# Reordering a two-block kernel: one normalised input for all projections, filter generation beside a matrix product, and intermediate results kept in memory

## The chip, the cores and the metric

The kernel runs on one core of a Trainium2 chip. The metric is device microseconds (us) of one execution. A core has a matrix engine (PE, with its weight loads PEld), a vector engine (DVE), a scalar engine (ACT), a second elementwise engine (POOL) and a sync engine (SP) from whose queue this kernel issues all its DMA transfers. SBUF is the on-chip memory of 128 partitions, PSUM the accumulators that PE writes, in eight banks of 128x512 float32.

## The reference

Two transformer-like blocks run one after the other on a sequence of 1024 tokens with 1024 channels, all in float32. The change lies almost wholly in the first sub-layer of the first block:

```
u    = rms_norm(x, norm_mix_g)
proj = u @ w_in                                   # 1536 Hyena + 1024 q,k + 512 v + 512 o + 16 gates
hy   = short_conv_centred(proj[:, :1536])         # 3 taps along time, per channel
spec = rfft(two_sided(filter_mlp(t) * exp(-t*|delta|)))  # 2 orders, 2 directions, 512 channels
z, g1, g2 = split(hy)
for o, gate in enumerate((g1, g2)):
    z = gate * (irfft(rfft(z, 2L) * spec[o])[:L] + z * skip[o])
y_hy = group_rms_norm(z, hy_norm_g)
qk   = silu(short_conv_centred(proj[:, 1536:2560]))
y_ml = sigmoid(o_pre) * (mlstm(q, k, v, i, f) + reversed mlstm(...))
h    = x + concat(y_hy, group_rms_norm(y_ml)) @ w_out
```

`filter_mlp` is two layers of sin(freq * (w z + b)) with 64 hidden units over 33 features of t, and a third product to 2048 channels. After this come cross attention and a feed-forward layer, and the second block: adaptive norms, dilated and sparse attention, and a gated feed-forward layer. In the second block the norm ahead of the feed-forward is `h2 = rmsnorm(x, g) * (1 + sc2) + sh2`.

## The kernel before

Every large product is made of three passes: a float32 operand is split into a rounded high part (made by ACT) and the rest (made by DVE or POOL), and PE adds high*high, high*low and low*high (`mm3`, L187, L188, L189). A product of 1024x1024 by a tile of 128 columns is 48 such instructions, 8 slices by 3 passes by 2 halves of 512.

The program is a row of stages. Each is a block in which every engine has its own instruction list; engines meet through semaphores (named signals) inside it, and a barrier of all engines stands between two blocks. Nothing of the next stage starts before all five engines have left the one before, but loads that SP has issued ahead go on. The order of the work is written out by hand.

The first sub-layer, by stage (`first_block`, L2695):

1. `phase_first_norm`: x is loaded, normalised and transposed into `xt`.
2. `phase_conv_proj` (L557): twelve tiles of 128 Hyena columns, transposed. Per tile ACT writes the middle tap (L621), DVE adds the two others from PSUM (L645, L647), and PE transposes the result back (L597).
3. `phase_filter_hidden` (L665): the hidden layers of the filter (PE L699, L706; DVE L717 to L726; ACT's sine). Beside it PE reverses the second half of the tokens with a permutation matrix (L694).
4. For each order o: `phase_filter_time` (L759) makes the filter taps (PE L789, each a float32 product of 64 rows), ACT the decay (L805), DVE their product (L838, L839), POOL sum and difference of the two directions (L861, L862), DVE the fold of the two halves (L825, with a copy of row 0 at L829), and both its rounded parts (L797, L817). Then `phase_filter_spectrum`, `phase_signal_spectrum` and `phase_inverse_gate` do the transforms as products with tables that are streamed in 256 KB units (`Tables`: ACT L901, POOL L906).
5. `phase_group_norm` on y_hy; beside it x is loaded a second time (4 MB).
6. `phase_row_norm`: x is normalised and transposed a second time, since `xt` has been overwritten.
7. `phase_qk_proj` (8 tiles), `phase_vo` (32 rows by halves), `phase_gates` (one tile for 16 gate columns), `phase_gate_scans` (logarithms on ACT, four scans on DVE L1623 and L1628, 16 transposes L1638).
8. `phase_mlstm`, whose first product is L1679, then `phase_mix` and the output projection.

In the second block `phase_rows_gemm_norm(..., modulated=...)` makes the output projection and, row block by row block, the next norm (`StreamNorm`: DVE scales at L360, PE turns). There the shift sh2 is added by PE: two products with a picking matrix into each bank (L371, L372), and the turning is four accumulating products (L378) in place of four transposes (L376).

## Time and profile before

| what | value |
|---|---|
| median of 3 runs | 4065.82 us (4064.43 to 4067.47) |
| the profiled execution, whole time | 4063.24 us |
| its span, first to last instruction | 4061.4 us |
| busy share PE, PEld, DVE, ACT, POOL | 89%, 70%, 49%, 28%, 13% |
| mean granted clock of PE | 0.937 of full speed |

The profile is one execution. Busy shares are means over very different stages. A slice of the page in which PE reads 6 or 7 tenths marks stages in which it waits; PEclk, the clock that was granted, falls in the same slices (0.5 is 1.2 GHz, 1.0 is 2.4 GHz). Idle time is put in brackets behind the instruction that ended it, with the instruction or transfer that released it. In the rows "rounded" is a high or low part, "plain" a float32 tile.

### The profile page before, as it was taken

How to read it: one execution, taken by the hardware profiler on the slowest of the kernel's cores; microseconds unless marked ns; L12 is line 12 of the kernel's file. 1: busy time of each engine (PE TensorE's matmuls, PEld its weight loads, DVE VectorE, ACT ScalarE, POOL GpSimd, SP SyncE). 2: the span in 40 equal slices, each digit the busy share in tenths (PEclk: the TensorE clock that was granted, in tenths of full speed). 3: DMA queues.
4: the chain of work that ended last, by engine and by line, in shares of the span. 5: the costliest groups of instructions: out<-in, count | busy, mean ns of one | idle time of the engine just before them, and what ended most of it. 6: DMA issues, size and time to landing. Idle time of an engine off the chain costs nothing. (4 is left out here: it accounts for less than half of the span.)

```text
span 4061.4 us, 43012 instructions
## 1 busy us (share of the span) xinstructions
PE 3631.5 (89%) x16474; PEld 2856.8 (70%) x16474; DVE 1998.9 (49%) x3148; ACT 1121.2 (28%) x2006; POOL 541.7 (13%) x377
## 2 busy tenths in 40 slices
PE   7868696896978879999999998889989899999998
PEld 6736475773667757788888775766668777888886
DVE  3264645314744143555553438789975433333243
ACT  3233232323333132211211324124445321111112
POOL 0046564000010000101100100000034201000000
PEclk8969798897989999999999999999999999999999
DMA  2012123100022111323221211100000211111111
GB/s 94 27 33 74 42 79 106 31 32 4 1 91 83 57 47 34 97 93 121 93 93 60 84 52 37 47 20 22 11 14 1 99 37 52 52 49 49 47 52 52
DMA packets 210515, 220.07 MB, mean 54 GB/s; under 512 B 15523, under 2 KB 148548, under 8 KB 210098
## 3 DMA queue, kind: packets, MB, share of 16 engines
q1 hardware_dynamic: 210356, 217.90, 16.9%
q8 instruction: 106, 1.74, 0.2%
q14 instruction: 53, 0.43, 0.0%
HBM read 205.79 MB, written 11.55 MB: 54 GB/s over the span
## 5 line engine op out<-in xcount | busy, mean ns | idle before, releaser
L187 PE MATMUL psum<-rounded,rounded 128*128 128x512 f32 (+2 forms) x3936 | 1544.7, 392 | 216.5 <-POOL rounded L906 86.0
L188 PE MATMUL psum<-rounded,rounded 128*128 128x512 f32 (+2 forms) x3936 | 1536.2, 390 | 0.0
L189 PE MATMUL psum<-rounded,rounded 128*128 128x512 f32 (+2 forms) x3936 | 1534.1, 390 | 0.0
L187 PEld LDWEIGHTS psum<-rounded,rounded 128*128 128x128 f32 x3936 | 752.0, 191 | 384.0 <-POOL rounded L906 90.8
L189 PEld LDWEIGHTS psum<-rounded,rounded 128*128 128x128 f32 x3936 | 751.4, 191 | 153.1
L188 PEld LDWEIGHTS psum<-rounded,rounded 128*128 128x128 f32 x3936 | 751.9, 191 | 150.2 <-issue 0.2
L2634 DVE TENSOR_TENSOR plain<-psum,plain 128x512 f32<-128x512 f32 x432 | 288.5, 688 | 112.0 <-PE psum L189 110.6
L2645 DVE TENSOR_TENSOR plain<-psum,plain 128x512 f32<-128x512 f32 x44 | 30.4, 692 | 437.3 <-ACT plain L2554 437.3
L3052 POOL TENSOR_TENSOR plain<-plain,plain 128x128 f32<-128x128 f32 (+3 forms) x64 | 89.4, 1408 | 717.4 <-ACT plain L3123 695.4
L2626 DVE TENSOR_TENSOR rounded<-plain,rounded 128x512 fp32r<-128x512 f32 x108 | 97.2, 900 | 174.8 <-ACT rounded L2543 174.7
L2915 DVE MAX8 plain<-plain 128x8 f32<-128x384 f32 (+5 forms) x192 | 170.6, 889 | 4.0
L2917 DVE MATCH_REPLACE8 plain<-plain,plain 128x384 f32<-128x384 f32 (+5 forms) x192 | 168.1, 876 | 0.0
L2554 ACT ACTIVATE plain<-psum 128x512 f32<-128x512 f32 x44 | 26.3, 599 | 470.3 <-PE psum L189 470.3
L2612 POOL TENSOR_TENSOR plain<-plain,plain 128x1024 f32<-128x1024 f32 x22 | 53.4, 2429 | 748.2 <-DMA plain<-in_w_down_dram 748.2
L2990 PE MATMUL psum<-plain,plain 64*128 64x512 f32 (+7 forms) x384 | 151.2, 502 | 0.0
L906 POOL TENSOR_TENSOR rounded<-plain,rounded 128x512 fp32r<-128x512 f32 x96 | 133.3, 1402 | 128.9 <-ACT rounded L901 128.7
L2600 POOL TENSOR_TENSOR plain<-plain 128x512 f32<-128x512 f32 x64 | 67.2, 1050 | 606.2 <-ACT plain L2556 606.2
L2556 ACT ACTIVATE plain<-psum 128x512 f32<-128x512 f32 x64 | 38.3, 598 | 380.3 <-PE psum L189 380.3
L2576 ACT ACTIVATE rounded<-plain 128x1024 fp32r<-128x1024 f32 x54 | 57.1, 1057 | 278.6 <-DMA plain<-in_ff_w_dram 160.6
L3071 DVE CUSTOM_DVE_ANT_0 plain<-psum,plain 128x128 f32<-128x128 f32 (+7 forms) x128 | 96.4, 753 | 69.1 <-PE psum L2990 38.1
L3125 ACT ACTIVATE plain<-plain,plain 128x128 f32<-128x128 f32 (+7 forms) x128 | 98.8, 772 | 56.7 <-DVE plain L3074 56.0
L901 ACT ACTIVATE rounded<-plain 128x512 fp32r<-128x512 f32 x96 | 58.7, 629 | 178.3 <-DMA plain<-in_c_fwd_dram 103.5
(284 smaller groups left out, 3935.8 us busy)
## 6 DMA issues: line engine op xcount, KB each, us to landing
plain<-in_ff_w_dram SPq DMA_DIRECT2D x64, 512.0 KB, 5.5
plain<-in_w_ada_dram SPq DMA_DIRECT2D x96, 256.0 KB, 3.1
plain<-in_w_gu_dram SPq DMA_DIRECT2D x44, 512.0 KB, 4.9
plain<-in_w_in_dram SPq DMA_DIRECT2D x36, 512.0 KB, 3.7
plain<-in_c_fwd_dram SPq DMA_DIRECT2D x64, 256.0 KB, 2.6
plain<-in_w_down_dram SPq DMA_DIRECT2D x22, 512.0 KB, 3.2
plain<-in_c_inv_dram SPq DMA_DIRECT2D x32, 256.0 KB, 2.6
plain<-in_x_dram SPq DMA_DIRECT2D x2, 4096.0 KB, 15.5
```

The costliest lines, as they stand in the source:

```text
L187: nc.tensor.matmul(out, wh, xh, start=first, stop=False)
L188: nc.tensor.matmul(out, wh, xl, start=False, stop=False)
L189: return nc.tensor.matmul(out, wl, xh, start=False, stop=last)
L906: self.core.nc.gpsimd.tensor_tensor(w.lo, w.raw, w.hi_raw, ALU.subtract).then_inc(S["ft_lo"].sem, 1)
L2626: nc.vector.tensor_tensor(ft[b].lo[:, f, cols], full[half], ft[b].hi_raw[:, f, cols], ALU.subtract).then_inc(S["ft_lo"].sem, 1)
L2634: nc.vector.tensor_tensor(hv, ps[:, 4 + t % 4, :], hv, ALU.add).then_inc(S["dve_free"].sem, 1)
L2915: nc.vector.max(best, sc).then_inc(self.done, 1)
L2917: nc.vector.match_replace(out=sc, in_to_replace=best, in_values=sc, imm_value=TAKEN).then_inc(self.done, 1)
L2990: last = nc.tensor.matmul(ps[:, 2 * (n % 2) + a // BANK, 0:b - a], q, k[:, a:b], start=True, stop=True)
L3052: nc.gpsimd.tensor_tensor(tb[n % 2][:, 0:w], biases[h % 2][:, L - w:L], sel_tile(core, i), ALU.add).then_inc(S["pool_done"].sem, 1)
L3071: nc.vector.tensor_tensor_reduce(out=sc[n % 2][:, 0:w], in0=pair(n, w), in1=b, scale=SCALE, scalar=-3.0e38, op0=ALU.add, op1=ALU.max, accu ...
L3125: nc.scalar.activation(sc[n % 2][:, 0:w], sc[n % 2][:, 0:w], ACT.Exp, bias=stat[:, n % 16, 1:2], accum_out=stat[:, n % 16, 2:3]).then_inc( ...
```

## The change

All products with `xt` now stand together right after the first norm: q and k with the gates as a ninth tile, then v and o with the scans beside them, then the convolution's projection with the filter generation beside it. What the mLSTM needs later (q, k, v, o, the running maximum, two column tables: `Kept`) is written to memory and loaded again during the second inverse transform and the group norm. The folded filters (2 x 4 MB) are also written to memory and loaded again, the first ahead of its spectrum, the second during the first inverse transform. The second load of x, its second norm, `phase_filter_hidden`, both `phase_filter_time`, `phase_gates` and `phase_gate_scans` are gone as stages. The reversal of the second half is made by reading PSUM backwards in the convolution, so the permutation products are gone. In the second block the shift is added by POOL (`StreamNorm.add`) in place of PE.

```diff
 def first_block(core):
+    phase_first_norm(core, x, xt, first_columns(core, weight_tiles(core, QK_RING_KB), w_rows, HY_COLS))
+    kept = Kept(core)
+    phase_qk_proj(core, xt, w_in, kept, first_pieces(core, VO_KB, w_rows[:, :, base:base + DH], count=1))
+    phase_vo(core, xt, w_in, kept, first_columns(core, weight_tiles(core, CONV_RING_KB), w_rows, 0))
-    phase_conv_proj(core, xt, w_in, hy)
-    phase_filter_hidden(core, hy)
+    filters = phase_conv_proj(core, xt, w_in, hy, kept)
     for o in range(2):
-        phase_filter_time(core, tables, o)
-        phase_filter_spectrum(core, tables, hy)
+        phase_filter_spectrum(core, tables, hy, filters.folds[0] if o == 0 else None)
         phase_signal_spectrum(core, tables)
-        phase_inverse_gate(core, tables, hy, o)
+        phase_inverse_gate(core, tables, hy, o, (lambda sp: load_folds(core, sp, filters.folds[1])) if o == 0 else (lambda sp: load_kept(core, sp, kept, True)))
-    phase_row_norm(core, x, xt, "norm_mix_g", 70, 74, [core.sig["x_ready"]], ...)
-    phase_qk_proj(core, xt, w_in, first_pieces(...))
-    phase_vo(core, xt, w_in)
-    phase_gates(core, xt, w_in)
-    phase_gate_scans(core)
     phase_mlstm(core)
```

The convolution's block, PE's list and DVE's list (F0 is 3, NF is 8):

```diff
@@ phase_conv_proj, tensor
                     for half in range(2):
                         last = mm3_cols(nc, ps[:, 2 * (n % 2) + half, :], ring[n % 4], ...)
+                        if half == 0 and 1 <= f <= NF:
+                            filters.taps(pe, f - 1, 1)
...
                     for t in range(TT):
-                        last = nc.tensor.transpose(ps[:, 4 + 2 * (m % 2) + t // 4, ...], tmp[m % 2][:, cuts[t]:cuts[t] + P], core.ident)
+                        last = nc.tensor.transpose(ps[:, 4 + t // 4, ...], tmp[m % 2][:, t * P:(t + 1) * P], core.ident)
+                if n < 2:
+                    filters.hidden(pe, n)
+                if 0 <= f < NF:
+                    filters.taps(pe, f, 0)
@@ phase_conv_proj, vector
+                if 1 <= f <= NF:
+                    filters.weigh(dve, f - 1, 1)
                 dve.wait_ge(S["act_done"].sem, S["act_done"].at(n + 1))
+                for out, src in ((t[:, 1:513], pr[:, 0:512]), (t[:, 513:L], pr[:, L - 2:511:-1])):
+                    last = nc.vector.scalar_tensor_tensor(out=out, in0=src, scalar=w0, in1=out, ...)
...
+                if 1 <= f <= NF:
+                    filters.fold(dve, f - 1)
+                if 0 <= f < NF:
+                    filters.weigh(dve, f, 0)
@@ class Filters
+    def taps(self, pe, f, m):
+        pe.wait_ge(S["windowed"].sem, S["windowed"].at(n))     # n = 2 * f + m
+        for half in range(2):
+            last = nc.tensor.matmul(ps[:, 6 + half, :], self.hid[...], self.w3[...], start=True, stop=True)
+        last.then_inc(S["tap_done"].sem, 1)
+    def store(self, sp, f):
+        sp.wait_ge(S["pair_folded"].sem, S["pair_folded"].at(f + 1))
+        sp.dma_start(self.folds[o]..., self.out).then_inc(S["fold_stored"].sem, 16)
```

The spectrum stage now makes the rounded parts of the folds itself, and the second block's norm adds its shift on POOL:

```diff
@@ phase_filter_spectrum
+            for n in range(4):                       # scalar
+                act.wait_ge(S["fold%d" % n].sem, S["fold%d" % n].at(16))
+                nc.scalar.activation(blocks(fold.hi, n), blocks(raw, n), ACT.Copy).then_inc(S["fold_hi"].sem, 1)
+            for n in range(4):                       # vector
+                nc.vector.tensor_tensor(blocks(fold.lo, n), blocks(raw, n), blocks(fold.hi_raw, n), ALU.subtract)...
@@ class StreamNorm
+    def add(self, pool, t, row):
+        pool.wait_ge(S["row_scaled"].sem, S["row_scaled"].at(t + 1))
+        nc.gpsimd.tensor_tensor(tmp, tmp, row, ALU.add).then_inc(S["row_added"].sem, 1)
```

How the lists move. DVE, one steady tile of the convolution before: the low part of a weight tile (L634), the two outer taps, and one copied column.

```order
L645 SCALAR_TENSOR_TENSOR plain_38400_1025_328<-psum,plain_896_128_50,plain_38400_1025_328 128x1023 [waits act_done]
L647 SCALAR_TENSOR_TENSOR plain_38400_1025_328<-psum,plain_896_128_50,plain_38400_1025_328 128x1023 [waits dve_chain]
L649 COPY plain_38400_1025_328<-plain_38400_1025_328 128x1 [waits dve_chain]
L634 TENSOR_TENSOR rounded_48640_1024_72<-plain_48640_1024_73,rounded_47616_1024_71 128x1024 [waits w_hi]
L645 SCALAR_TENSOR_TENSOR plain_39488_1025_329<-psum,plain_896_128_50,plain_39488_1025_329 128x1023 [waits act_done]
```

The same engine and place in the changed kernel, from one `act_done` to the next (L872 and L875 are the outer taps in halves, L713 the fold, L684 and L685 the taps times the decay, L852 the low part):

```order
L872 SCALAR_TENSOR_TENSOR plain_38400_1024_1473<-psum,plain_896_128_50,plain_38400_1024_1473 128x512 [waits act_done]
L872 SCALAR_TENSOR_TENSOR plain_38400_1024_1473<-psum,plain_896_128_50,plain_38400_1024_1473 128x511
L875 SCALAR_TENSOR_TENSOR plain_38400_1024_1473<-psum,plain_896_128_50,plain_38400_1024_1473 128x513 [waits dve_chain]
L875 SCALAR_TENSOR_TENSOR plain_38400_1024_1473<-psum,plain_896_128_50,plain_38400_1024_1473 128x510
L713 TENSOR_TENSOR plain_35328_2048_1488<-plain_30208_2048_1485 128x512 [waits fold_stored,pair_summed]
L713 TENSOR_TENSOR plain_35328_2048_1488<-plain_30208_2048_1485 128x512 x3
L684 TENSOR_TENSOR plain_32256_2048_1486<-psum,plain_34304_1024_1487 128x512 [waits pair_summed,tap_done,decay_ready]
L685 TENSOR_TENSOR plain_32256_2048_1486<-psum,plain_34304_1024_1487 128x512
L852 TENSOR_TENSOR rounded_43776_1024_64<-plain_43776_1024_65,rounded_42752_1024_63 128x1024 [waits w_hi]
L684 TENSOR_TENSOR plain_32256_2048_1486<-psum,plain_34304_1024_1487 128x512 [waits pair_summed,tap_done,decay_ready]
L685 TENSOR_TENSOR plain_32256_2048_1486<-psum,plain_34304_1024_1487 128x512
```

Four instructions per tile have become thirteen, and the first L684 pair is what the signal `windowed` tells PE.

PE in the second block's norm before, the end of one row block's turning and the products behind it (L371 and L372 add the shift, L378 turns):

```order
L378 MATMUL psum<-plain_0_896_49,plain_5632_2048_9062 128x128 x4
L371 MATMUL psum<-rounded_51072_8_21830,rounded_50816_128_21828 128x512
L372 MATMUL psum<-rounded_51072_8_21830,rounded_50944_128_21829 128x512
L378 MATMUL psum<-plain_0_896_49,plain_5632_2048_9062 128x128 x4
L187 MATMUL psum<-rounded_42496_2048_9617,rounded_17920_8192_21649 128x512
```

PE at the same place in the changed kernel (L387 is a transpose, L190 the first of the three passes):

```order
L192 MATMUL psum<-rounded_42496_2048_9295,rounded_26112_8192_21328 128x512
L387 MATMUL psum<-plain_0_896_49,plain_5632_2048_8740 128x128 [waits row_added,row_lo]
L387 MATMUL psum<-plain_0_896_49,plain_5632_2048_8740 128x128 x7
L190 MATMUL psum<-rounded_42496_2048_9295,rounded_17920_8192_21327 128x512
```

The four shift products per row block are gone from PE, and its turning waits for POOL's `row_added` where it waited for DVE's `row_scaled`.

## Rows read from the trace of the kernel before

**Rows 1.** Busy time by stretch: window, length, PE, PEld, DVE, ACT, POOL, PEclk, DMA, GB/s.
```profile
42.00:184.00 142.00, 141.80 (x662) 118.22 (x663) 42.54 (x45) 32.13 (x32) 0.00 (x0) 0.99 0.11 30
...
445.40:506.30 60.90, 27.67 (x32) 10.49 (x32) 47.04 (x59) 17.27 (x28) 27.95 (x19) 0.52 0.08 26
506.30:672.00 165.70, 148.30 (x630) 121.43 (x630) 70.19 (x85) 51.71 (x89) 103.15 (x71) 0.94 0.24 72
672.00:729.50 57.50, 21.78 (x114) 19.20 (x113) 41.59 (x57) 22.85 (x37) 8.03 (x8) 0.63 0.36 120
729.50:819.40 89.90, 89.90 (x384) 73.86 (x384) 26.25 (x21) 22.43 (x21) 0.00 (x0) 0.97 0.12 36
...
828.90:918.60 89.70, 89.67 (x384) 73.77 (x384) 6.88 (x3) 15.77 (x19) 0.00 (x0) 0.97 0.07 24
918.60:969.60 51.00, 15.51 (x66) 12.39 (x65) 17.25 (x11) 9.36 (x9) 0.99 (x2) 0.67 0.07 7
```

**Rows 2.** Timeline of PE: start, length, instruction, count [idle before <-releaser].
```profile
224.53 15.72 PE L789 MATMUL psum<-plain,plain 64*128 64x512 f32 x18 [8.76 <-DMA plain<-in_hy_filt_w_dram]
...
277.57 0.80 PE L187 MATMUL psum<-rounded,rounded 128*128 128x512 f32 x1 [25.37 <-POOL rounded L906]
...
394.83 0.80 PE L187 MATMUL psum<-rounded,rounded 128*128 128x512 f32 x1 [13.00 <-POOL rounded L906]
...
686.80 7.38 PE L1241 MATMUL psum<-plain,plain 128*128 128x128 f32 x48 [14.78 <-DVE plain L1214]
...
963.34 1.96 PE L1638 MATMUL psum<-plain,plain 64*128 64x64 f32 x16 [21.84 <-DVE plain L1629]
...
969.60 3.78 PE L1679 MATMUL psum<-plain,plain 64*128 64x512 f32 x4 [4.29 <-DMA plain<-in_c_sel_dram]
```

**Rows 3.** Timeline of PE, the convolution's transposes of tiles 0, 1 and 10.
```profile
65.64 1.03 PE L597 MATMUL psum<-plain,plain 128*128 128x128 f32 x8
...
77.43 1.03 PE L597 MATMUL psum<-plain,plain 128*128 128x128 f32 x8
...
183.40 1.03 PE L597 MATMUL psum<-plain,plain 128*128 128x128 f32 x8
```

**Rows 4.** Timelines of PE and DVE in the two filter stages.
```profile
212.07 3.70 PE L694 MATMUL psum<-plain,plain 128*128 128x512 f32 x8
...
242.21 0.41 DVE L829 COPY plain<-plain 1x512 f32<-1x512 f32 x1
...
248.61 4.62 DVE L825 TENSOR_TENSOR plain<-plain 128x512 f32<-128x512 f32 x4 [1.19 <-POOL plain L862]
...
270.37 2.48 DVE L825 TENSOR_TENSOR plain<-plain 128x512 f32<-128x512 f32 x4
```

**Rows 5.** DMA issues: tile, queue, count, KB each, us to landing.
```profile
plain<-in_x_dram SPq DMA_DIRECT2D x1, 4096.0 KB, 13.8
...
saved_x<-plain SPq DMA_DIRECT2D x8, 512.0 KB, 2.6
```

**Rows 6.** Timelines of POOL and DVE, where one stage hands over to the next.
```profile
676.31 4.04 POOL L1201 TENSOR_TENSOR plain<-plain 128x512 f32<-128x512 f32 x4 [7.76 <-POOLq L1094]
...
690.88 4.94 DVE L1225 TENSOR_TENSOR plain<-psum,plain 128x512 f32<-128x512 f32 x9
...
826.59 2.29 DVE L1557 TENSOR_TENSOR rounded<-plain,rounded 128x2048 fp32r<-128x2048 f32 x1 [3.30 <-ACT rounded L1530]
```

**Rows 7.** Timelines of DVE (second block) and PE (first block), and the page's POOL group.
```profile
3274.36 1.28 DVE L360 SCALAR_TENSOR_TENSOR plain<-plain,plain,plain 128x1024 f32<-128x1024 f32 x1
...
3280.55 1.28 DVE L360 SCALAR_TENSOR_TENSOR plain<-plain,plain,plain 128x1024 f32<-128x1024 f32 x1
...
1237.12 1.03 PE L376 MATMUL psum<-plain,plain 128*128 128x128 f32 x8
...
1240.75 1.03 PE L376 MATMUL psum<-plain,plain 128*128 128x128 f32 x8
...
L2612 POOL TENSOR_TENSOR plain<-plain,plain 128x1024 f32<-128x1024 f32 x22 | 53.4, 2429 | 748.2 <-DMA plain<-in_w_down_dram 748.2
```

731 lines of the change are left out of this document (390 added, 341 removed).

## The prediction, on record before the changed kernel ran

> **What bounds the kernel now.** I read the page first: PE is busy 89% of the span, no other engine over half, and its idle time stands in the slices of the first quarter. The busy times by stretch come next [rows 1]. In the long products (42 to 184, 729.5 to 819.4, 828.9 to 918.6) PE is busy all the time at a clock of 0.97 to 0.99, so nothing can be won there but fewer instructions. Between them lie stretches in which PE works half the time or less at 0.5 to 0.67. The timeline of PE then says what ended each wait [rows 2]: a DMA, the last table unit of POOL, the DVE of a norm, the scans. So the first 970 us are a row of full products with gaps between, and the price of a stage is either its PE time or, where PE waits, its whole length, since a barrier closes it. The chain of waits on the page agrees: it is nearly all PE.
>
> **The sum, as a new timetable.** I lay the changed stages end to end up to the mLSTM's first product, which starts at 969.6 now [rows 2]. Behind it only one place changes.
>
> 1. The first norm stays: 42.0.
> 2. q and k: eight tiles took 89.9 [rows 1], so nine take 89.9 * 9/8 = 101.1. The gates' own stage goes. Its small loads are first in SP's queue and are wanted six tiles later. The spills of q and k sit in the same queue ahead of the loads for v and o, but each tile's 512 KB store lands in about 2.6 [rows 5] and a tile lasts 11.2. At 143.1.
> 3. Gap to v and o. It was 9.5: last tile's taps and silu, then ACT's and DVE's parts of the first weights, the latter 2.29 [rows 6]. Now only two bias additions stand behind the last product, so 7.4. At 150.5.
> 4. v and o: 89.7 [rows 1], to 240.2. The scans filled the wait of 21.84 in [rows 2]; with the logarithms they are some 19 us on ACT and DVE. DVE does them ahead of the third piece of weights, which PE wants some 45 us after the start, half the stage. Hidden; if that cover failed the price would be up to 21.84.
> 5. Gap to the convolution: its first tiles are loaded ahead, so one ACT and one DVE part of 1024 columns and the barrier, 4. At 244.2.
> 6. The convolution's own 142.0 [rows 1]; tile to tile is 77.43 - 65.64 = 11.79 [rows 3]. PE gets 32 tap products and 4 hidden ones. Four such float32 products took 3.70 at the full clock [rows 4], 0.9 each, against 15.72 / 9 = 1.75 each at half clock in the old filter stage [rows 2]. That is 36 * 0.9 = 32.4 and 1 for the 16 transposes: 33.
>    Waits of PE inside it: the taps of one half need the banks that DVE frees with its product `windowed`. After a tile's last product, ACT writes the middle tap (1.3), DVE adds the outer ones (2.6), folds the pair before (2.48 for four [rows 4]) and only then multiplies (1.3): 7.7. PE comes back to those banks after 0.8 of transposes, 1.8 of taps and half a tile, 5.5: 8.1. So it just fits. The two pairs with copied rows need 4 * 0.41 more [rows 4] and some waits, about 2 each past the fit. I take 5 in all. Lower bound 0. Upper bound: the reversed PSUM reads are in no row. If they ran at half speed, DVE and ACT would need 1.8 more per tile, and if POOL shared DVE's time in the fold it would be 4.62 for 2.48 [rows 4]: 2 more; with the first 5 that is 8 * 3.8 + 5 = 35. I take 5, since the scans before also read backwards and nothing on POOL runs at the time of the fold. So 142 + 33 + 5 = 180, to 424.2.
> 7. Gap to the first spectrum. Taps and fold behind the last tile 6.5; the last 1 MB store, by 512 KB in 2.6 [rows 5], 5; barrier; then table units and the first quarter of the fold, 2 MB, by the 4 MB that landed in 13.8 [rows 5] about 7.5; ACT's and DVE's parts of 2048 columns 1.9 and 2.29 [rows 6]. That is 24. Bounds 18 (store and loads in half the time) and 36 (store at the 4 MB transfer's whole latency). At 448.2.
> 8. The three transform stages of order 0 keep their 445.4 - 277.6 = 167.8 [rows 1, 2], to 616.0. The load of the second fold, 4 MB, now stands ahead of the table units in SP's queue. The inverse starts PE at 394.83 [rows 2], with four units there; the stage began some 2.3 before, the first unit's rounding on ACT and POOL. 4 MB are down 13.8 later [rows 5], about 406, then the fifth unit, ACT and POOL 4 more: 410, and PE takes its fifth unit at about 411. So 0, at most 8 per inverse if the written memory reads slower.
> 9. Gap to the second spectrum. It was 60.9 [rows 1]. Of it 4.3 remain for the gate and the barrier, as 676.31 against 672.0 in the second order [rows 6], then three table units on ACT 1.7, the fold's high and low part 4.2 and 1 for POOL beside it: 11.3. The clock falls to 0.5 before every such start now too [rows 1, 2], so its price is in the old stages already. At 627.3.
> 10. Order 1: 165.7 [rows 1], to 793.0. The load of q, k ahead of its inverse is like that in 8.
> 11. Group norm until DVE's last row, 690.88 + 4.94 [rows 6], and the start: 696.3 - 672.0 = 24.3. 4.7 MB are loaded beside it where x's 4 MB took 13.8; issued near 676.5 they are there by 693. At 817.3.
>
> 969.6 - 817.3 = 152.3 us. Where it comes from: the second norm with its hand-over 35, gates and scans about 40, the first pair of filter stages about 30 (94 to 24 and 38 more of PE), the second about 50.
>
> 12. Second block. A row block of the modulated norm takes 3280.55 - 3274.36 = 6.19, one in the plain norm 1240.75 - 1237.12 = 3.63 [rows 7]; PE has no idle time in either, so the four shift products and the slower turning cost 2.56 per row. POOL's addition is 128x1024, 2.43 [rows 7], and lies between DVE's scaling and PE's turning. In the six rows beside products PE has two rows of slack for it. The last two rows are turned with nothing beside them: there PE saves as much again, about 5, and the addition costs that back, once at the first turning and once at the last. Best case 6 * 2.56 = 15, worst 0 if POOL and DVE slow each other as in [rows 4], where four folds took 4.62 beside POOL and 2.48 alone. I take 11.
>    The Trainium skill, SBUF — State Buffer, "Who interferes with whom", says that a DVE instruction with two SBUF inputs and a GpSimd instruction that reads SBUF exclude each other for the whole instruction. The 4.62 against 2.48 agrees in direction. By that rule a scaling that meets an addition waits it out, 1.28 + 2.43 = 3.7 a row, still under 6.19; by it the sum would hardly change unless DVE's other work does not fit either, which is the rival below.
>
> Together 163.3. Against the profiled execution, 4063.24 - 163.3 = 3899.9; it ran 2.6 under the median of the runs, so 3902.5, and I say 3902.
>
> **Rivals.**
> A. The convolution is paced by DVE. For it: thirteen instructions a tile where four stood, and the fit of 8.1 against 7.7 in step 6. Against it: DVE was busy 42.54 of 142 there [rows 1] and gets about 53 more, 8 * (2.5 + 2.6) for folds and windows and 12 for the hidden layers, on 180. Price 35 for my 5: 3902 + 30 = 3932.
> B. The reloads are late. For it: 12 MB more through one queue, twice ahead of the table stream. Against it: the 13.8 for 4 MB. Step 7 at 36, 8 for each inverse, 4 in the group norm: 12 + 16 + 4 = 32, so 3934.
> C. POOL's addition gives nothing in the second block: DVE waits for POOL in each row and the row stays near 6. The POOL and DVE rows above speak for it, the row's 3.7 against it. 3902 + 9 = 3911.
> D. Better than forecast: step 6 without waits, step 7 at 18, step 12 at 15: 3902 - 5 - 6 - 4 = 3887.
> E. Slower than before. One mechanism: the ring taps, window, addition, fold, store, in which each link waits for the next before its buffers are free. If it ran serially, PE would stand for each of the 16 half pairs. It would have to lose 163 / 16 = 10.2 us at each to undo the gain. The old filter stage, which is this ring on its own, needed 277.57 - 224.53 = 53 for eight half pairs with its low parts, 6.6 each [rows 2], so even wholly exposed it costs about 106, and the time would be near 4000. Only store and reload at several times the measured durations would carry it over 4066.
> F. The change does not do what it says: a stage that I count as gone still costs. The order of SP, PE and DVE leaves no room for it.
>
> **How the numbers follow.** Main forecast 3902 with its own range of 3888 to 3916: 0.60. A 0.09, B 0.11, both together in part 0.03 (up to 3950). C 0.06. D 0.09. E 0.01 for over 4066, and 0.01 for an exposed ring that still gains. The range 3880 to 3934 leaves out a little over one in ten. A measurement of this kernel can tell 0.2%, 8 us. Every case but E's first half is far below 4058: faster 0.985, same 0.005, slower 0.01.
>
> **What would show it.** PE's first convolution product after v and o near 244, the first spectrum near 448, the second near 627, the mLSTM's first product near 817. In the convolution, tiles with taps 15.3 to 15.8 apart; a wait of PE on `windowed` (the DVE product L685) of over 1 us in most tiles is A. A wait for a fold or table transfer in either inverse is B. In the second block turnings 3.7 to 4.3 apart; near 6 is C. The forecast is wrong if the gaps of steps 7 and 9 sum to over 50, or if the clock in the long products falls below the 0.97 of now.

## The result

The changed kernel takes 3914.41 us (median of four runs, 3911.34 to 3921.62), the kernel before 4065.7. The ratio on record is 0.9632, with a 95% interval of 0.962 to 0.9643 (the two medians alone give 0.9628). The forecast was 3902 us with a range of 3880 to 3934, so the time lies inside it, 12 us above the 3902. Measured once more, five runs beside the version at the end of the experiments, the kernel after took 3914.98 (3913.14 to 3922.1); one of these is what is called its second profile below.

The profiled execution took 3914.14 us with a span of 3912.3; before it was 4063.24 and 4061.4. So 149.1 us are to be accounted for, where the prediction said 163.3.

### The profile page after: what moved, and what is told of

Same layout as the page of the kernel before. It is cut to its first block and busy times, and to the rows that moved or that the text cites. A ratio compares the mean times of both kernels' runs of the same rounds, so it can differ in the third digit from the quotient of the medians.

```text
span 3912.3 us, 42554 instructions
## 1 busy us (share of the span) xinstructions
PE 3565.9 (91%) x16290; PEld 2817.0 (72%) x16290; DVE 1961.9 (50%) x3111; ACT 1093.4 (28%) x1949; POOL 550.7 (14%) x385
## 5 line engine op out<-in xcount | busy, mean ns | idle before, releaser
L190 PE MATMUL psum<-rounded,rounded 128*128 128x512 f32 (+2 forms) x3936 | 1546.1, 393 | 186.9 <-POOL rounded L933 37.7
L190 PEld LDWEIGHTS psum<-rounded,rounded 128*128 128x128 f32 x3936 | 751.2, 191 | 366.5 <-POOL rounded L933 40.2
## 6 DMA issues: line engine op xcount, KB each, us to landing
plain<-fold SPq DMA_DIRECT2D x8, 1024.0 KB, 10.1
```

Of the source, the lines that this page charges most:

```text
L190: nc.tensor.matmul(out, wh, xh, start=first, stop=False)
```

## The profile after

The busy time by stretch, as in [rows 1] (window, length, PE, PEld, DVE, ACT, POOL, granted clock, DMA share, GB/s). In the order of time: q, k and gates; v and o with the scans; the convolution with the filters; the gap to the first spectrum; the gap between the two orders; the group norm up to the mLSTM; and, last, the second block's output projection with its norm.

```profile
41.90:142.20 100.30, 100.28 (x432) 82.48 (x432) 30.07 (x24) 25.67 (x24) 0.00 (x0) 0.98 0.25 75
...
149.40:239.60 90.20, 90.18 (x384) 74.05 (x384) 19.56 (x10) 21.49 (x24) 0.00 (x0) 0.97 0.25 85
...
243.40:427.40 184.00, 181.28 (x746) 129.90 (x747) 95.92 (x138) 51.98 (x65) 45.66 (x34) 0.99 0.22 73
427.40:452.80 25.40, 2.71 (x17) 2.07 (x15) 7.51 (x9) 9.03 (x9) 3.71 (x3) 0.59 0.61 226
620.30:631.20 10.90, 0.03 (x1) 0.03 (x1) 6.96 (x7) 6.66 (x6) 3.72 (x3) 0.63 0.07 24
800.70:824.80 24.10, 8.29 (x50) 8.12 (x49) 19.60 (x31) 1.63 (x2) 8.02 (x8) 0.65 0.54 201
3048.70:3158.20 109.50, 99.50 (x448) 81.44 (x448) 44.89 (x45) 23.94 (x49) 27.98 (x10) 0.95 0.23 82
```

The gaps are what to look at. Before, TensorE stood or ran at half clock for 60.9 us between the orders; now it is 10.9. Of the stretch of 57.5 between the second order and q, k [rows 1] the 24.1 of the group norm are left, and the one of 51.0 with the gate products and scans is gone. VectorE, busy for 42.54 of 142.0 in the old convolution, is busy for 95.92 of 184.0 in the new one, and TensorE is still busy for 181.28.

The waits of TensorE from there to the mLSTM, which answer to [rows 2] (start, length, instruction, count, idle time before and what ended it):

```profile
321.99 1.98 PE L666 MATMUL psum<-plain,plain 64*128 64x512 f32 x4 [1.36 <-DVE plain L685]
387.64 1.98 PE L666 MATMUL psum<-plain,plain 64*128 64x512 f32 x4 [1.36 <-DVE plain L685]
452.78 0.79 PE L190 MATMUL psum<-rounded,rounded 128*128 128x512 f32 x1 [19.14 <-DVE rounded L1039]
...
569.04 0.79 PE L190 MATMUL psum<-rounded,rounded 128*128 128x512 f32 x1 [12.30 <-POOL rounded L933]
585.97 0.50 PE L190 MATMUL psum<-rounded,rounded 128*128 128x512 f32 x1 [1.69 <-POOL rounded L933]
631.17 0.79 PE L190 MATMUL psum<-rounded,rounded 128*128 128x512 f32 x1 [10.91 <-DVE rounded L1039]
...
766.37 0.50 PE L190 MATMUL psum<-rounded,rounded 128*128 128x512 f32 x1 [1.54 <-POOL rounded L933]
824.78 1.95 PE L1754 MATMUL psum<-plain,plain 64*128 64x512 f32 x4 [1.04 <-PEq L1248]
```

Only two of the sixteen tap pairs wait (L666, before 321.99 and 387.64), 1.36 us each; a float32 product stands in two records, so a pair counts x4. The mLSTM's first product stands at 824.78 and stood at 969.60 [rows 2]: 144.8 us earlier.

The transfers of the folded filters, from the page (instruction, count, KB each, us to landing):

```profile
fold<-plain SPq DMA_DIRECT2D x8, 1024.0 KB, 4.7
plain<-fold SPq DMA_DIRECT2D x8, 1024.0 KB, 10.1
```

And the second block's norm: VectorE's scaling (L363), POOL's addition (L369) and TensorE's turning (L387), which answer to [rows 7].

```profile
3122.86 1.28 DVE L363 SCALAR_TENSOR_TENSOR plain<-plain,plain,plain 128x1024 f32<-128x1024 f32 x1
3125.58 2.15 DVE L363 SCALAR_TENSOR_TENSOR plain<-plain,plain,plain 128x1024 f32<-128x1024 f32 x1
...
3135.19 1.28 DVE L363 SCALAR_TENSOR_TENSOR plain<-plain,plain,plain 128x1024 f32<-128x1024 f32 x1
...
3151.51 2.20 DVE L363 SCALAR_TENSOR_TENSOR plain<-plain,plain,plain 128x1024 f32<-128x1024 f32 x1
```
```profile
3124.30 2.35 POOL L369 TENSOR_TENSOR plain<-plain,plain 128x1024 f32<-128x1024 f32 x1 [41.71 <-DVE plain L363]
...
3150.28 2.34 POOL L369 TENSOR_TENSOR plain<-plain,plain 128x1024 f32<-128x1024 f32 x1 [2.60 <-DVE plain L363]
```
```profile
3126.80 1.06 PE L387 MATMUL psum<-plain,plain 128*128 128x128 f32 x8 [2.11 <-POOL plain L369]
3130.46 1.03 PE L387 MATMUL psum<-plain,plain 128*128 128x128 f32 x8
3135.47 1.06 PE L387 MATMUL psum<-plain,plain 128*128 128x128 f32 x8 [1.24 <-POOL plain L369]
...
3152.77 1.94 PE L387 MATMUL psum<-plain,plain 128*128 128x128 f32 x8 [3.88 <-POOL plain L369]
3156.28 1.94 PE L387 MATMUL psum<-plain,plain 128*128 128x128 f32 x8 [1.56 <-POOL plain L369]
```

The turnings stand 3.5 to 5.0 apart, where row blocks stood 6.19 apart [rows 7], and from the first product to the end of the last turning the stage takes 109.5 where it took 117.7 (3191.3 to 3309.0). TensorE waits for POOL at five of the eight, 2.11 + 1.24 + 1.20 + 3.88 + 1.56 = 10.0 us (the 1.20, at 3144.14, falls into the gap of the rows shown).

## The experiments

Two questions were put first. Which part of the change gives how much? And what paces the new convolution, TensorE or the ring of taps, window, addition and fold?

### The shift on POOL alone

The kernel before with one part of the change (cut at the dots):

```diff
@@ class StreamNorm
+    def add(self, pool, t, row):
+        pool.wait_ge(S["row_scaled"].sem, S["row_scaled"].at(t + 1))
+        nc.gpsimd.tensor_tensor(tmp, tmp, row, ALU.add).then_inc(S["row_added"].sem, 1)
...
+        if self.added:
+            pe.wait_ge(S["row_added"].sem, S["row_added"].at(t + 1))
+        else:
+            pe.wait_ge(S["row_scaled"].sem, S["row_scaled"].at(t + 1))
...
-    norm = StreamNorm(..., BEHIND, shift=shift and shift.operands())
+    norm = StreamNorm(..., BEHIND, added=modulated is not None)
...
-                    pe.wait_ge(S["shift_lo"].sem, S["shift_lo"].at(1))
```

> The kernel before, with one part of the change alone: in the second block's modulated norm POOL adds the shift to the scaled rows, and TensorE's four shift products per row are gone. Theory (the parts add up, and nothing that happens before the second block touches this one): the stretch from the second block's output projection to the end of its norm shortens by the same 8.2 us as between the two profiles, so 4065.8 - 8.2 = 4057.6 us, ratio 0.9980. The turnings of the last rows stand 3.7 to 5 us apart. Rival 1 (POOL and VectorE slow each other so much that only the full change, whose DMA queues look different, gains): within 2 us of the kernel before. Rival 2 (what the prediction took, 11 us of 15): 4054.8 us. All the rest of the 151 us gained, about 143, must then be the new order of the first block.

Measured: 4060.3 us (11 runs) against 4065.79, ratio 0.9987, interval 0.9978 to 0.9996. The busy time of the same stretch, of this kernel and of the kernel before:

```profile
3197.05:3306.50 109.45, 99.46 (x448) 81.36 (x448) 44.86 (x45) 23.94 (x49) 28.00 (x10) 0.95 0.23 81
```
```profile
3191.30:3309.00 117.70, 117.17 (x544) 93.03 (x544) 43.48 (x46) 24.17 (x51) 8.97 (x2) 0.98 0.20 72
```

The stage shortens by 8.25 us, as much as in the full change, with the same waits in the same places. TensorE's busy time falls by 17.7 for the 96 records that are gone, and 9.5 of that come back as waiting for POOL. The time as a whole fell by 5.5, and the interval reaches from 1.6 to 8.9, so it takes in the 8.2 (0.9980) and leaves out the 11 of rival 2; that rival 1, 2 us at most, falls is shown by the stage, hardly by the interval. In the profiled execution this kernel was already 5.7 us late at this first product, 3.4 of it from an earlier stage, the one that begins at 1401.56 (1399.20 in the kernel before), where its instructions are those of the kernel before: 115.6 at a granted clock of 0.91 against 112.3 at 0.94. The kernel after takes 115.1 there, and 112.5 in two of the runs below, so this is a difference of one execution to the next. The first theory stands. The rest of the 149.1, some 141, must come from the first block's new order.

### The filters behind the convolution instead of beside it

```diff
-    FIRST = 3
+    FIRST = 12
...
-                        if half == 0 and 1 <= f <= NF:
-                            filters.taps(pe, f - 1, 1)
...
+            for f in range(NF + 1):
+                if f >= 1:
+                    filters.weigh(dve, f - 1, 1)
+                    filters.fold(dve, f - 1)
+                if f < NF:
+                    filters.weigh(dve, f, 0)
```

> The kernel after, but with all taps, windows, additions and folds of the filters behind the convolution's last tile instead of beside tiles 3 to 11; the two hidden layers stay beside. Same instructions, buffers and stores. Theory (beside the tiles the ring costs only TensorE's own time for the products, about 31 us of tap pairs, and on its own it costs its full latency): one pair then needs window product 1.3, tap pair 1.93, window product 1.3, POOL's two additions about 2.6, fold 2.5 and the hand-overs about 0.4, together 10 us; 8 pairs 80 us. The tiles' part falls by 31 us of taps, 3 of waits and 2 of interruptions to about 148. So 3914 + 80 - 36 = 3958 us. Rival 1 (the price of an exposed ring as in the prediction, 6.6 us per half pair, 106 in all): 3914 + 106 - 36 = 3984 us. Rival 2 (it matters little where the ring stands, the gain was all in the dropped stages and their starts): within 8 us of 3914.

Measured: 3977.94 us, ratio 0.9784 (0.9769 to 0.9799), so 63.5 more than the kernel after, where the theory said 44 and rival 1, with the prediction's price of an exposed ring, 70. It is nearer to the rival. Rival 2 falls. The two parts, tiles alone and ring alone, by stretch:

```profile
242.50:388.50 146.00, 145.98 (x676) 118.74 (x677) 55.94 (x70) 40.15 (x48) 0.00 (x0) 0.99 0.14 40
396.00:490.20 94.20, 60.33 (x65) 18.52 (x64) 39.56 (x66) 13.74 (x18) 38.30 (x32) 0.50 0.22 81
```

And three tap pairs in the ring:

```profile
401.17 3.78 PE L666 MATMUL psum<-plain,plain 64*128 64x512 f32 x4 [1.45 <-DVE plain L685]
...
414.48 3.78 PE L666 MATMUL psum<-plain,plain 64*128 64x512 f32 x4 [4.31 <-DVE plain L685]
...
425.99 3.78 PE L666 MATMUL psum<-plain,plain 64*128 64x512 f32 x4 [2.52 <-DVE plain L685]
```

The ring alone takes 94.2, not 80. The missing term is the clock: the granted clock is 0.50 over the whole stretch, the 1.2 GHz level, and a tap pair takes 3.78 instead of 1.98. The theory's chain has one tap pair in each of its eight turns; with 3.78 for its 1.93 it gives 80 + 8 * 1.85 = 94.8. That is a sum that fits, no run had the ring alone at the full clock. Of the 16 pairs 14 wait for VectorE's window product, as expected, 1.44 at one half and 2.52 or 4.31 at the other; the first waits for nothing and one for the second half of the taps' weights, 3.62. TensorE is busy for 60.33 of the 94.2, at half speed.

The tiles end with the transposes of tile 10 at 389.45, 146.93 after their first product; in the kernel after it is 427.24 - 243.36 = 183.88. So beside the tiles the ring costs 36.95 us, and apart it costs 94.2 and a gap of 23.55 for 19.14. The same work in another place is worth a good 60 us (271.2 - 209.4 = 61.8 from the convolution's first product to the first spectrum's). It is the largest part of the gain that a run cut out. The rest of the first block, some 80 us (the second norm, the gates and scans as stages of their own, the starts between them), is read from the stretches that have gone or become shorter in the table; no run took it apart.

### Twice the tap products

```diff
-        for half in range(2):
+        for half in (0, 0, 1, 1):
             last = nc.tensor.matmul(ps[:, 6 + half, :], ...)
```

> The kernel after, with every one of the 32 tap products issued twice in a row into the same bank. Theory (TensorE is what paces the convolution with its filters): 16 more pairs at the measured 1.93 us each, 30.9, less up to 2.7 for the two waits of 1.36 us that VectorE's longer cycle removes: 28 to 31 us more, 3942 to 3945 us. The tile distance rises from about 16.05 to about 19.9. Rival (rival A of the prediction, VectorE's thirteen instructions pace it): half or more of the extra TensorE work disappears into waits, under 16 us more, below 3930 us.

Measured: 3936.48 us, ratio 0.9678 (0.9663 to 0.9693), 22 more than the kernel after. The first of TensorE's doubled pairs in one tile and in the next:

```profile
353.94 3.70 PE L666 MATMUL psum<-plain,plain 64*128 64x512 f32 x8
...
373.47 3.70 PE L666 MATMUL psum<-plain,plain 64*128 64x512 f32 x8
```

A doubled pair takes 3.70, and no wait of 1 us is left. From one tile to the next it is 373.47 - 353.94 = 19.53, against 16.05 in the kernel after (346.54 - 330.49 there): 3.48 for two more pairs. So a second pair right behind the first costs 1.74, not the 1.93 that I had taken from the whole interruption. By that the sum is 16 * 1.74 - 2.7 = 25.1; from the convolution's first product to the first spectrum's the trace has 234.54 against 209.42, 25.1. The 22 of the medians lies within their spread. TensorE paces the convolution; rival A of the prediction would have hidden most of this. The expectation's lower end, 28, was missed by the size of a pair.

That also splits the price of the taps. Without them a tile takes 11.79 [rows 3], with them 16.05: 2.13 for each pair. 1.74 are the products, by the price of the second pair, and 0.39 are left for the interruption of the long rounded products. What in the interruption costs them, no run shows.

### The window product later

```diff
                 if 0 <= f < NF:
+                    dve.wait_ge(S["tap_done"].sem, S["tap_done"].at(2 * f + 1))
+                    dve.wait_ge(S["decay_ready"].sem, S["decay_ready"].at(2 * f + 1))
+                    for at, width in ((146, 512), (148, 512), (197, 256)):
+                        nc.vector.tensor_tensor(core.view(at, width), ps[:, 6, 0:width], filters.decay[:, 0, 0:width], ALU.mult)
                     filters.weigh(dve, f, 0)
```

> The kernel after, with three more VectorE products (128x512, 128x512, 128x256, about 0.62 + 0.62 + 0.35 = 1.6 us) ahead of the first window product of each of the 8 pairs; their results are used by nobody. Theory (in six of the eight tiles the window product is ready only 0.4 us before TensorE wants its banks; in the other two TensorE already waits 1.36): TensorE waits 1.2 us more in six tiles and 1.6 in two, 6 * 1.2 + 2 * 1.6 = 10.4, so 3914 + 10 = 3924 us (3921 to 3928), and a wait of about 1.2 us on L685's successor shows in every tile. Rival (there is real slack, and the two waits are only the copied rows): the extra work hides, 2 * 1.6 = 3 us at most, 3914 to 3917 us.

Measured: 3926.57 us, ratio 0.9662 (0.9647 to 0.9677), 12 more. TensorE's waits, in a tile with copied rows and in one without:

```profile
323.48 1.98 PE L666 MATMUL psum<-plain,plain 64*128 64x512 f32 x4 [2.89 <-DVE plain L685]
...
342.28 1.98 PE L666 MATMUL psum<-plain,plain 64*128 64x512 f32 x4 [1.08 <-DVE plain L685]
```

The added products delay TensorE by 1.08 in a tile without copied rows, and by 2.89 - 1.36 = 1.53 in one with them, where no slack was left. So the fit is real, and its slack is 1.53 - 1.08 = 0.45 us a tile. The prediction had 8.1 against 7.7 for it.

The sum of the expectation comes near the measured 12 in part by luck. Only five tiles without copied rows wait, not six; the first pair of all does not. And the two tiles with copied rows grow by 3.1, from 17.5 to 20.6, though their wait grew by 1.5. The rest is the clock. Behind the wait of 2.89 TensorE's long products run near the lower level for 3.7 us:

```profile
325.40:329.10 3.70, 3.70 (x11) 2.91 (x11) 1.29 (x2) 0.00 (x0) 3.70 (x4) 0.57 0.00 0
```

The granted clock is 0.57 there; in the kernel after, behind its wait of 1.36, it is 1.00 (324.0 to 327.7).

### The window product ahead of the fold

This kernel and the next three have one execution each. The kernel after lies between 3911 and 3922 us in its own nine, so a total that is 2 to 6 us lower says little; the readings go by the traces.

```diff
-                if 1 <= f <= NF:
-                    filters.fold(dve, f - 1)
                 if 0 <= f < NF:
                     filters.weigh(dve, f, 0)
+                if 1 <= f <= NF:
+                    filters.fold(dve, f - 1)
```

> The kernel after, with VectorE's order in the convolution's tile turned round: the next pair's first window product stands ahead of the fold of the pair before, not behind it. Theory (the two waits of TensorE of 1.36 us on L685, at 322.0 and 387.6 of the kernel after, come from the fold with its four copied rows that stands ahead of the product): both waits go, the convolution takes 184.0 - 2.7 = 181.3 us from its first product to the last, no wait on L685 over 0.5 us is left. Rival (the product is late for another reason, the tail of VectorE's taps): the waits stay at 1 us or more, or others come up since POOL's additions now wait for the later fold.

Measured: one run at 3908.55 us. VectorE in one tile, now with the window product (L685 is its second half) ahead of the fold (L713):

```profile
332.19 0.68 DVE L685 TENSOR_TENSOR plain<-psum,plain 128x512 f32<-128x512 f32 x1
332.79 2.49 DVE L713 TENSOR_TENSOR plain<-plain 128x512 f32<-128x512 f32 x4
```

No tap pair waits any more. The tile-10 transposes stand 423.40 - 242.68 = 180.72 behind the first product instead of 183.88, 3.2 less where 2.7 was said, and the first spectrum 207.04 behind it instead of 209.42. The theory holds; the two waits were the fold's copied rows. In the kernel after such a fold lasts from 316.46 to 320.73, 4.27 for the 2.49 of a plain one; less the slack of 0.45 that makes 1.33, and the wait is 1.36.

### The gap to the first spectrum

The last store of the fold is waited for only ahead of the third quarter of the reload, and table units and quarters are loaded and rounded in turns:

```diff
-            sp.wait_ge(S["fold_stored"].sem, S["fold_stored"].at(16 * NF))
...
     for n, q in enumerate(FOLD_ORDER):
+        if all_stored is not None and n == 2:
+            sp.wait_ge(core.sig["fold_stored"].sem, all_stored)
+        if tables is not None:
+            sp.dma_start(tables.ring[n].raw, core.ap["c_fwd"][n]).then_inc(tables.loaded[n], 16)
         sp.dma_start(raw[:, 4 * q:4 * q + 4, :], ...)
...
-            for u in range(3):
-                tables.high(act, u)
             for n in range(4):
+                if n < 3:
+                    tables.high(act, n)
```

> The kernel after, with two edits in the gap to the first spectrum (25.4 us, which the prediction put at 24 by a sum of a store, a barrier and 2 MB of loads). First, the last 1 MB store of the fold is not waited for at the end of the convolution, only ahead of the reload's third and fourth quarter. Second, the first three table units and fold quarters are issued, and rounded on ScalarE, in turns instead of all units first. Theory (the gap is that chain of transfers): 4 us go with the store's wait and 2 to 3 with the order, the gap is 18 to 20 us. Rival (the gap is the barrier and the engines' roundings, the transfers are beside them): less than 2 us.

Measured: one run at 3912.39 us. From tile 10's transposes to the first spectrum it is 449.21 - 428.11 = 21.10, in the kernel after 452.78 - 427.24 = 25.54. That is 4.4 less, where the theory said 6 to 7 and the rival under 2: the chain of transfers is right as a cause and the size is off. (In the second profile of the kernel after the gap is 26.18.) The two edits were not run apart. ScalarE in this kernel, first table unit and first quarter:

```profile
441.69 0.63 ACT L928 ACTIVATE rounded<-plain 128x512 fp32r<-128x512 f32 x1 [6.78 <-DMA plain<-in_c_fwd_dram]
444.92 1.91 ACT L1021 ACTIVATE rounded<-plain 128x2048 fp32r<-128x2048 f32 x1 [2.61 <-DMA plain<-fold]
```

And what all transfers moved, in 40 slices of 0.875 us from 425 to 460:

```profile
GB/s 0 0 0 0 0 0 0 0 0 0 0 0 49 384 386 211 194 403 330 262 335 377 449 431 396 417 461 405 393 435 433 375 84 0 0 59 241 0 0 0
```

The loads no longer wait for the store, and from the 13th slice to the 33rd the transfers have no pause. The first quarter's rounding starts 16.8 us behind tile 10's transposes instead of 21.25 (448.49 in the kernel after). With the wait gone, the bytes ahead of the first quarter remain, at the rate that the slices show.

Three more things stand in this trace, and the first two reach the last kernel below. The second quarter of the fold is now late for TensorE, by 0.87 at 455.79. The rounding in turns also shortens the gap to the second spectrum, from 10.91 to 9.09. And the convolution took 1.4 more, one of its tiles 19.1 instead of 17.5, since behind the second wait of 1.36 (at 386.91) the clock fell:

```profile
388.90:392.60 3.70, 3.70 (x10) 2.88 (x11) 1.29 (x2) 0.00 (x0) 3.70 (x4) 0.54 0.22 76
```

The granted clock is 0.54 there and 1.00 in the same place of the kernel after. It fell in the run of the reloads in pieces too (0.54). So a wait inside the long products can cost as much again as it lasts, in some executions and not in others.

### The reloads in pieces

```diff
-            ahead(sp)
-            tables.load(sp, ap["c_inv"], ap["c_fwd"] if o == 0 else None)
+            tables.load(sp, ap["c_inv"], ap["c_fwd"] if o == 0 else None, ahead)
...
             sp.dma_start(self.ring[u % 4].raw, src).then_inc(self.loaded[u % 4], 16)
+            if u - 4 < len(between):
+                between[u - 4](sp)
```

> The kernel after, with the 4 MB reloads in the two inverse transforms issued in pieces, one behind each of the first table units, instead of whole ahead of the fifth unit. Theory (rival B of the prediction in small: TensorE's waits of 1.69 at 586.0 and 1.54 us at 766.4 are the table units queued behind the reload): both waits fall under 0.3 us, the two inverses together take 3 us less. Rival (they are the start of the table stream itself, since the rounding has to begin anew in every stage): both waits stay above 1 us.

Measured: one run at 3908.33 us. Both waits are gone. The stretch from the inverse's first product to the next stage, for either order, in this kernel and in the kernel after:

```profile
570.12:630.28 60.16, 49.25 (x210) 40.33 (x211) 23.49 (x24) 16.44 (x23) 35.17 (x26) 0.93 0.42 142
747.29:811.47 64.18, 49.40 (x211) 40.43 (x211) 29.47 (x33) 11.44 (x19) 39.62 (x31) 0.90 0.50 176
```
```profile
569.04:631.17 62.13, 49.54 (x210) 40.28 (x210) 25.80 (x24) 16.31 (x23) 36.03 (x26) 0.91 0.39 138
749.21:815.47 66.26, 49.95 (x210) 40.51 (x210) 29.61 (x33) 11.27 (x19) 40.21 (x31) 0.89 0.47 168
```

1.97 and 2.08 less, 4.05 together. Against the second profile of the kernel after, whose two waits are 0.63 and 1.45 and whose stretches are 61.50 and 66.04, it is 1.34 and 1.86. So the fifth table unit did stand behind the reload, and the price of whole reloads is 1.3 to 2.1 us an inverse.

### The addition in halves

```diff
-        nc.gpsimd.tensor_tensor(tmp, tmp, row, ALU.add).then_inc(S["row_added"].sem, 1)
+        for q in range(2):
+            part = tmp[:, q * BANK:(q + 1) * BANK]
+            nc.gpsimd.tensor_tensor(part, part, row[:, q * BANK:(q + 1) * BANK], ALU.add).then_inc(S["row_added"].sem, 1)
...
         for q in range(2):
+            if self.added:
+                pe.wait_ge(S["row_added"].sem, S["row_added"].at(2 * t + q + 1))
```

> The kernel after, with POOL's addition of 128x1024 in two of 128x512, each released to TensorE by itself. TensorE waits for POOL at five of the eight turnings of the second block's norm, 2.11 + 1.24 + 1.20 + 3.88 + 1.56 = 10.0 us. Theory (it waits for the end of the addition, so half of it, 1.2 us, goes at each): 5 to 6 us less, the stage from the output projection's first product to the end of the last turning takes 104 us instead of 109.5. Rival (VectorE and POOL exclude each other on their shared operands: VectorE's scalings then meet one of two POOL instructions more often, and some of the gain is eaten): 2 to 3 us less.

Measured: one run at 3909.95 us; the stage took 107.67 from its first product to the last turning's end (3048.01 to 3155.68), 1.8 less than 109.5. Theory and rival both asked for more. TensorE's first row in halves, POOL's addition and VectorE's second scaling:

```profile
3124.82 0.63 PE L389 MATMUL psum<-plain,plain 128*128 128x128 f32 x4 [1.03 <-POOL plain L371]
3125.96 0.66 PE L389 MATMUL psum<-plain,plain 128*128 128x128 f32 x4 [0.50 <-POOL plain L371]
```
```profile
3123.40 2.50 POOL L371 TENSOR_TENSOR plain<-plain,plain 128x512 f32<-128x512 f32 x2 [41.50 <-DVE plain L363]
```
```profile
3124.69 2.30 DVE L363 SCALAR_TENSOR_TENSOR plain<-plain,plain,plain 128x1024 f32<-128x1024 f32 x1
```

The first half starts 1.3 earlier against the stage's first product, but the row ends when the second half of the addition and then half a turning have ended: 0.72 behind the addition (3126.62 against 3125.90) instead of 1.21 (3127.86 against 3126.65). By the ends of the turnings the three waited rows among the products gain 0.3 to 0.6 each, and the last two rows 0.6 together. I had counted the earlier start as the gain.

### All four together

> The kernel after with the four edits of the runs above together: VectorE's window product ahead of the fold, the last store of the fold behind the first reloads, table units and fold quarters in turns, the reloads of the inverses in pieces behind the first table units, POOL's addition in halves. By their own traces they take 2.4 (first spectrum minus the convolution's first product, 209.42 to 207.04), 4.4 (the gap to the first spectrum, 25.54 to 21.10), 2.0 + 2.1 (the two inverses up to the next stage) and 1.8 us (the second block's output projection up to the next stage), 12.7 together. Theory (each waits on the path for itself, so they add up): 3914.4 - 12.7 = 3901.7 us, ratio to the kernel before 0.9596. Rival (the edits share what they gain, since the DMA queues are full at 380 to 450 GB/s in the gap): half of it, 3908 us.

> The kernel after once more, in the same rounds on the same chip as the version with the four edits, so that these two can be compared. Expected as in the first measurement, 3914.4 us, 3911 to 3917.

Measured: 3903.97 us (3899.83 to 3906.3), ratio to the kernel before 0.9602 (0.9589 to 0.9615); the kernel after in the same rounds 3914.98, ratio 0.9634 (0.9621 to 0.9647). This version beats both kernels, by 11.0 us the one after. The theory of a plain sum said 12.7, with a rival of about 6. One wait shows where part of the rest may be: the second quarter of the fold comes late behind the first.

```profile
444.27 0.79 PE L190 MATMUL psum<-rounded,rounded 128*128 128x512 f32 x1 [14.67 <-DVE rounded L1064]
450.86 0.50 PE L190 MATMUL psum<-rounded,rounded 128*128 128x512 f32 x1 [1.59 <-DVE rounded L1064]
```

From the convolution's first product to the mLSTM's it is 572.55 instead of 581.42, 8.9 less where the parts had 10.9. Up to the first spectrum nothing is lost, 202.18 instead of 209.42, 7.2 for the parts' 6.8. Behind it the sum had left out two things that both stand in the run of the gap alone: this wait (0.87 there, 1.59 here, 0.45 more in the second order) and the shorter gap to the second spectrum (9.08 for 10.91), which nearly cancel. The other 2 us are spread over the transform stages, which differ by about 1 us each between the two profiles of the kernel after; what they are is not shown.

## Why the prediction was right, and where its 14 us are

**The timetable to the mLSTM** (steps 1 to 11) said 817.3 and came out at 824.8. Steps 1 to 5 are within 0.8 each and end at 243.4 where 244.2 was said: norm 41.9, q, k and gates 100.3, gap 7.2, v and o 90.2, gap 3.8. The logarithms and scans are hidden entirely, as step 4 said: no wait of TensorE in that stage.

**Step 6, the convolution, is the largest miss up to there**, 184.0 for 180. Its waits were over-estimated (2.7 for 5) and its products under-estimated, so the two errors took something from each other. The term "36 * 0.9 = 32.4 and 1 for the 16 transposes" is the mis-sized one. Sixteen pairs cost 2.13 each, 34.1, where 32 * 0.9 = 28.8 stood, because 0.39 come with each interruption; doubling the taps showed that the products alone are 1.74. The hidden layers and transposes cost 146.93 - 141.4 = 5.5 where 4.6 stood, 141.4 being the same stretch before (42.0 to 183.40 [rows 1, 3]). The reversed reads of PSUM, which the prediction had in no row, are no slower than it took: the two outer taps last 1.41 each, 2.8 for the 2.6 of its sum. The mechanism was right: TensorE paces it, the window product fits by 0.45 us, the copied rows do not. The tiles stand 16.05 apart, not the 15.3 to 15.8 of the forecast, and rival A is refuted by the doubled taps, which did not disappear into waits, and by the two waits where it asked for one in most tiles.

**Step 7, the gap,** took 25.4 for 24, with the last store landing at about 439 and the first quarter's rounding at 448.49. Rival B was right in kind in steps 8 and 10, in a size of 1.3 to 2.1 us an inverse instead of 8. Step 8 still gave 167.5 for 167.8, step 9 gave 10.9 for 11.3.

**Step 10, the second order,** took 169.5 for 165.7. 1.54 are the wait at 766.37. Most of the rest is the clock: after the three starts of this order TensorE's products are at full speed 5.7, 4.9 and 3.9 us later, in the old second order, from which the 165.7 were taken, 3.5, 3.8 and 3.1 us later. Half of the 4 between them is lost, about 2. The prediction had the fall before every start in its old stages, but not that its end moves.

It moves from one execution to the next. In the first order of this profile the three are 3.2, 3.2 and 3.1. In the second profile of the same kernel it is the first order that is late, with 6.0, 5.1 and 3.9, and the second has 3.9, 4.0 and 3.5. From the second order's first product to the transposes of the group norm it took 184.3 in one profile and 182.5 in the other, with 180.5 in the kernel before. So about 2 us of this step's miss are this execution's.

```profile
452.80:458.50 5.70, 5.67 (x17) 4.26 (x18) 5.26 (x3) 4.41 (x4) 0.11 (x1) 0.73 0.24 101
631.20:637.00 5.80, 5.80 (x14) 4.56 (x15) 5.80 (x3) 2.73 (x3) 2.65 (x1) 0.51 0.00 0
```
```profile
452.70:458.40 5.70, 5.70 (x13) 4.46 (x14) 5.24 (x3) 4.44 (x4) 0.09 (x1) 0.50 0.10 42
632.20:638.00 5.80, 5.78 (x18) 4.66 (x19) 5.80 (x3) 2.78 (x3) 2.66 (x1) 0.67 0.00 0
```

These are the first 5.7 and 5.8 us of the same stage in both orders, in the first profile and in the second: granted clock 0.73 and 0.51, then 0.50 and 0.67. What sets the moment of its return is open.

**Step 11** gave 24.1 for 24.3.

**Step 12, the second block,** gave 8.2 for 11. TensorE's busy time fell by 17.7 and its idle time rose by 9.5. The prediction had 15 + 5 of saving, 5 for the additions, and took 4 off for doubt. So the saving was over-estimated by 2, and the term for the additions is the mis-sized one, 9.5 for 5; the 4 for doubt covered most of both. One addition was named at the first turning, where the wait is 2.11, and one at the last, where the last two rows wait 3.88 + 1.56 = 5.4; the waits of 1.2 at two rows between them were not counted. The turnings are 3.5 to 5.0 apart, where 3.7 to 4.3 was said; rival C asked for near 6. (Its price, 9, should have been the 11 that the sum has for this step.)

On the exclusion of VectorE and POOL the trace decides now. A scaling takes 1.28 alone, and four of the eight began during an addition. Two began more than 1 us before its end and took 2.15 and 2.20. The first ended 1.08 after the addition did (3125.58 + 2.15 against 3124.30 + 2.35), the second 1.09 (3151.51 + 2.20 against 3150.28 + 2.34), and the one in the run with halves 1.09 as well (3126.99 against 3125.90). The other two began only 0.1 before its end (3135.19 and 3143.91), took 1.28 and ended 1.14 and 1.19 after it. So however long the two overlap, at most 0.2 of the 1.28 pass beside the addition. That is what the Trainium skill says, SBUF — State Buffer, "Who interferes with whom": such a pair excludes each other for the whole instruction. It costs 0.9 us twice here.

**Between the mLSTM and the second block** 2.2 us of the 144.8 are lost (142.6 earlier at the second block's output projection, 3048.70 against 3191.31), in stages whose code is unchanged. The kernel with the shift alone loses 3.4 over the same stages, and the stage that took 112.3 in the kernel before and 115.1 in the kernel after takes either 112.5 or about 115 in the other profiles. So I put it down to the execution; another 1.7 go the same way behind the second block's norm (150.75 earlier at the next stage, 149.1 at the end). The ledger of the 163.3 - 149.1 = 14.2: 7.5 up to the mLSTM, 2.2 and 1.7 in unchanged stages, 2.8 in the second block.

## What to carry to other kernels

Work that waits on itself belongs beside the longest stretch of long products there is: the same ring cost 37 us beside the tiles and over 94 alone, part of it because TensorE ran at the lower clock there. When TensorE is lent out in small pieces, price the interruption with the product: 2.13 us a pair here for products of 1.74, and read it from the distance between tiles. A wait that these pieces bring into the long products can cost the clock as well, about 1.6 us behind a wait of 1.36 or 2.89 in three of the runs. Before a difference between two stages is called a property of the stage, look at a second execution. Before moving work to POOL, count who waits for it in every row and which VectorE instruction it will stop; a part taken from both ends of a wait pays only for what then ends earlier, not for what starts earlier.

## What the runs showed of the hardware that was not expected

- In the ring alone the granted clock was 0.50, the lower level, over the whole 94.2 us. Before it the engine had run its long products at full speed and then waited 3.55 us for the last tile's transposes (at 394.04); within it pauses of 1.4 to 4.3 us stood between the pairs.
- Behind a wait of 2.89 us inside the convolution's long products the clock was 0.57 for 3.7 us. Behind a wait of 1.36 it stayed at 1.00 in the kernel after and was 0.54 in two other kernels at the same place.
- Under the same instructions the clock came back 3.2 us after the first spectrum's start in one execution of the kernel after and 6.0 us in another.
- Memory written by the kernel is read back without a penalty that shows: in the gap to the first spectrum, in the row of slices above, fold and table together moved at 262 to 461 GB/s from the 18th slice to the 32nd. x's 4 MB in 13.8 us [rows 5] are 304 GB/s. That a quarter's 10.1 us to landing are mostly its place among the others is a reading; no run loads one alone.
- A VectorE scaling that meets a POOL addition ends 1.08 to 1.19 us after it, in all four meetings of the kernel after. The other way round it is alike: in the convolution POOL's sum at 337.74 begins beside VectorE's low part L852 (337.57 to 338.79) and takes 2.17, where the next takes 1.29.
